# A windowed attention step over both key groups, on half-array tiles

## Chip, cores and metric

The kernel runs on one core of a Trainium2 chip. The metric is the device time of one execution in microseconds (us). Engines are named as in the profile: PE is TensorE (PEld its weight loads), DVE VectorE, ACT ScalarE, POOL GpSimd, SP SyncE, which here issues most DMAs.

## What is computed

A trunk of two layers on one sequence of 1024 tokens, width 1024. Layer 0 mixes tokens by windowed attention, layer 1 by a gated MLP; each is followed by a dense squared-ReLU MLP. The change lies in the attention of layer 0, cut to its core here (CHUNK = 64, 16 chunks, 16 query heads of 64, 2 key heads, so 8 query heads for each; a chunk's queries see their own chunk and the one before, 128 keys):

```
q, k, v = split(h @ w_qkv)
q = rope(rms_norm(q, q_gain), positions);  k = rope(rms_norm(k, k_gain), positions)
scores = einsum('bnqhgd,bnkhd->bnhgqk', q, kk) * HEAD_DIM ** -0.5     # kk: chunk n-1 and n
m = maximum(max(scores), sink)
p = exp(scores - m)
probs = p / (sum(p) + exp(sink - m))
o = einsum('bnhgqk,bnkhd->bqhd', probs, vv)
return o @ w_o
```

## The kernel before

Activations lie transposed, features on partitions and tokens on the free axis. Products with weights are made of three terms from a high and a low part of each operand (w_hi, w_lo, h_hi, h_lo); the inner products of the attention itself are plain fp32. A weight block of 128 output features is a "unit" (`unit`, matmuls at L1404). SP loads it to w_raw, ACT splits off w_hi (L455), POOL w_lo (L381). Units come in pairs. Unit 0 gives k, units 1 to 8 four pairs of q, unit 9 gives v; units 10 to 17 are the output projection, which needs the finished attention in h_hi and h_lo.

A pair j of q holds four heads, its first halves in one unit, its second in the other. DVE turns it by the rotary angles (`turn`, L1098 to L1110), multiplies by the spread head norms (L1117, L1118) and signals q_cs. SP then writes it to q_dram in eight DMAs (`save_q`, L330), since the attention wants heads side by side and the head dimension on partitions. Pairs 0 and 1 are the heads of key group 0, 2 and 3 those of group 1.

The attention is a pipeline of 32 steps t, step t being chunk n = t // 2 and group g = t % 2, with semaphores between engines and the order on each engine written by hand in its `step`:

- SP: `load_q` loads one tile qf, 64 partitions by 512 (8 heads x 64 tokens), for step t once the scores of t - 2 are done; two tiles. All 32 loads stand behind all saves.
- PE: `scores(t+1)` (L1570): four fp32 matmuls with K = 64 rows, stationary 128 queries of two heads, moving 128 keys, into PSUM tile pp[0] or pp[3] (`score_tile`); it waits for the exps of t - 1. `mix` of step t - 3 (L1589): one matmul, moving pt (128 keys x 512 queries), stationary a 128x128 window v_w that holds the values of group g in its own half and zeros in the other, so that both groups add up in one PSUM bank of 128 partitions. `turn` of step t - 2 (L1580): four transposes of the probabilities into pp[1].
- DVE: maxima (L1139), sums and reciprocal of t - 1 (L1128, L1130), the copy of transposed probabilities to pt for group 0 (L1147), the low part of the output once per chunk (L1152). The sinks are written once as a column behind each score row (L1170) and stay there, as each PSUM tile belongs to one group.
- ACT: four exps (L617), the copy to pt for group 1 (L626), the high part of the output (L630), the copy to v_w (L637).
- POOL: normalises the probabilities (L394).

The loop has its first eight and last four steps as straight code, the others in a hardware loop. Ahead of it PE transposes v (L1559), ACT copies that (L605), and DVE waits for all saves of q.

Of the kernel before, what the change touches and what calls it, by code (L numbers as in the profile page):

```python
# [13 lines left out]
S = 1024  # L14
# [22 lines left out]
U_K, U_Q, U_V = 0, 1, KC + 1  # L37
U_WO = KC + 2
# [26 lines left out]
def build(nc, x_in, c_in, pos_in, weights, mod_w, cols, mats, ws_in, bias_in, q_dram, v_dram, out):  # L65
# [5 lines left out]
    with ctx:  # L71
# [31 lines left out]
        with ExitStack() as attn:  # L103
            kf = sb("kf", [HD, KV, PAD + S], f32, attn)
            vt = sb("vt", [P, PAD + S], f32, attn)
            v_s = sb("v_s", [P, NCH, P], f32, attn)
            with ExitStack() as rope:
# [4 lines left out]
                oa = sb("oa", [P, 2, S], f32, rope)  # L112
                ob = sb("ob", [P, 2, S], f32, rope)
            qf = sb("qf", [HD, 2, HALF], f32, attn)
            pr = sb("pr", [P, 4, 4, P + 1], f32, attn)
            pt = sb("pt", [P, 2, HALF], f32, attn)
            v_w = sb("v_w", [P, 2, 3 * P], f32, attn)
            small = sb("small", [P, 4, 4, 4], f32, attn)
# [68 lines left out]
        qf_in = [sem("qf_in0"), sem("qf_in1")]  # L187
# [3 lines left out]
        vw, pv_mm, o_hi, o_lo = (sem(n) for n in ("vw", "pv_mm", "o_hi", "o_lo"))  # L191
        sinks_in, vw_zero = sem("sinks_in"), sem("vw_zero")
# [35 lines left out]
        def score_tile(g):  # L228

            return (pp[0], pp[3])[g][:, :].rearrange("p (a c) -> p a c", a=2)[:, :, 0:2 * (P + 1)].rearrange(  # L230
                "p a (b k) -> p a b k", b=2)

# [39 lines left out]
        def _(sp):  # L272
# [51 lines left out]
            def save_q(j):  # L324

                sp.wait_ge(q_cs, 2 * j + 2)
                for i in range(4):
                    head = 4 * (j % 2) + i
                    for part, src in ((0, oa), (1, ob)):
                        sp.dma_start(q_dram[:, j // 2, 32 * part:32 * part + 32, head, :].rearrange("n d t -> d n t"),  # L330
                                     src[32 * i:32 * i + 32, 1 - j % 2, :].rearrange("d (n t) -> d n t", t=CHUNK)).then_inc(q_out[j], 16)

            with sp.Fori(1, 4) as pair:
                for s in range(2):
                    load_block(pair, s, -1)
            save_q(0)
            load_block(4, 0, -1)
# [4 lines left out]
            save_q(2)  # L342
            save_q(3)

            def load_q(t, n, g):
                if not static(t) or t >= 2:
                    sp.wait_ge(sc_mm, t - 1)
                sp.dma_start(qf[:, g, :], q_dram[n, g]).then_inc(qf_in[g], 16)

            for j in range(4):  # L350
                sp.wait_ge(q_out[j], 16 * 8)
            sp.wait_ge(k_roped, 2)
            for g in range(KV):
                load_q(g, 0, g)
            with sp.Fori(1, NCH) as n:
                for g in range(KV):
                    load_q(n * 2 + g, n, g)
# [20 lines left out]
        def _(pool):  # L378
# [5 lines left out]
            nc.gpsimd.memset(kf[:, 0, 0:PAD], 0.0).then_inc(pads, 1)  # L384
            nc.gpsimd.memset(kf[:, 1, 0:PAD], 0.0).then_inc(d_lo, 1)
            nc.gpsimd.memset(vt[:, 0:PAD], 0.0).then_inc(pads, 1)
            pool.wait_ge(pads, 2)
# [62 lines left out]
        def _(act):  # L450
# [125 lines left out]
            for j in range(4):  # L576
# [7 lines left out]
                if j == 0:  # L584
                    act.wait_ge(k_roped, 2)
                    for g in range(KV):
                        for part in range(2):
                            act.dma_start(kf[32 * part:32 * part + 32, g, PAD:],
# [20 lines left out]
            def exps(t, b):  # L609

                lo = PAD if static(t) and t < 2 else 0
                sc = score_tile(b % 2)
                act.wait_ge(p_max, t + 1)
                if not static(t) or t >= 4:
                    act.wait_ge(p_tr, t - 3)
# [5 lines left out]
            def probs_copy(t, n):  # L621

                act.wait_ge(p_tr, t + 1)
                if not static(t) or t >= 2:
                    act.wait_ge(pv_mm, t - 1)
                nc.scalar.activation(pt[:, 1, :], pp[1][:, HALF:], ACT.Copy).then_inc(p_cp[1], 1)  # L626

            def out_high(n, e):
                act.wait_ge(pv_mm, n * 2 + 2)
                nc.scalar.activation(h_hi[:, :, bass.ds(n * CHUNK, CHUNK)],  # L630
                                     pp[2][:, HALF * e:HALF * e + HALF].rearrange("p (h t) -> p h t", t=CHUNK),
                                     ACT.Copy).then_inc(o_hi, 1)

            def window(n, e):
                if not static(n) or n >= 2:
                    act.wait_ge(pv_mm, n * 2 - 2)
                nc.scalar.activation(v_w[:, e, :].rearrange("p (g c) -> p g c", g=2)[:, :, 0:HD],  # L637
                                     v_s[:, bass.ds(n, 1), :].rearrange("p a (g c) -> p (a g) c", g=KV),
                                     ACT.Copy).then_inc(vw, 1)

            def step(m, b):

                t = m * 4 + b
                if not static(t) or t < 2 * NCH:
                    exps(t, b % 4)
                    if b % 2 == 0:
                        window(m * 2 + b // 2, (b // 2) % 2)
                if b % 2 and (not static(t) or 3 <= t < 2 * NCH + 2):
                    probs_copy(t - 2, m * 2 + ((b - 1) // 2 - 1))
                if b % 2 == 0 and (not static(t) or t >= 4):  # L650
                    out_high(m * 2 + (b // 2 - 2), (b // 2) % 2)

            act.wait_ge(v_cp, 4)
            act.wait_ge(vw_zero, 1)
            for m in range(2):
                for b in range(4):
                    step(m, b)
            with act.Fori(2, NCH // 2 - 1) as m:
                for b in range(4):
                    step(m, b)  # L660
            for b in range(7):
                step(NCH // 2 - 1, b)
# [211 lines left out]
        def _(dve):  # L874
# [217 lines left out]

            for j in range(4):
# [17 lines left out]
                if j == 1:  # L1111
                    mod_part(2)
                if j < 3:
# [7 lines left out]
            mod_part(3)  # L1121


            def sums(t, b):
                dve.wait_ge(p_exp, t + 1)
                if not static(t) or t >= 4:
# [5 lines left out]
            def maxima(t, b):  # L1132

                lo = PAD if static(t) and t < 2 else 0
                sc = score_tile(b % 2)
                dve.wait_ge(sc_mm, t + 1)
                if lo:
                    V.memset(pr[:, b, :, 0:lo], 0.0)
# [3 lines left out]
            def probs_copy(t, n):  # L1142

                dve.wait_ge(p_tr, t + 1)
                if not static(t) or t >= 2:
                    dve.wait_ge(pv_mm, t - 1)
                V.tensor_copy(pt[:, 0, :], pp[1][:, 0:HALF]).then_inc(p_cp[0], 1)  # L1147

            def out_low(n, e):
                cs = bass.ds(n * CHUNK, CHUNK)  # L1150
                dve.wait_ge(o_hi, n + 1)
                V.tensor_tensor(out=h_lo[:, :, cs],  # L1152
                                in0=pp[2][:, HALF * e:HALF * e + HALF].rearrange("p (h t) -> p h t", t=CHUNK),
                                in1=h_hi[:, :, cs].bitcast(f32), op=ALU.subtract).then_inc(o_lo, 1)

            def step(m, b):
                t = m * 4 + b
                if not static(t) or t < 2 * NCH:
                    maxima(t, b % 4)
                if not static(t) or 1 <= t < 2 * NCH + 1:  # L1160
# [659 lines left out]
```

## Time and profile before

| | us |
|---|---|
| median of 3 runs | 2422.3 (2419.77 to 2426.09) |
| profiled execution | 2425.68 |
| its span, first to last instruction | 2423.9 |
| mean granted clock of PE | 0.979 of full speed |
| PE busy | 2313.5 (95%) |
| DVE, ACT, POOL busy | 1222.3, 670.5, 771.4 |
| last q turned to first scores | 200.1 to 214.3 |
| first scores to output projection | 214.3 to 314.1 |

The span holds all instructions of one execution; the rest of its time lies outside. A busy PE isn't a PE at its peak, as a matmul record includes its way through the array and records overlap. So durations of PE work are best read as the distance from start to start. The granted clock says which share of 2.4 GHz the chip gave PE. The attention takes a small part of the span; most is the dense products on both sides of it.

### The profile page before, as it was taken

To read this page: it belongs to the slowest core of one execution; us is meant where nothing else is said; L and a number is where in the kernel's file an instruction comes from. 1 tells how busy PE (TensorE), PEld (TensorE's weight loads), DVE (VectorE), ACT (ScalarE), POOL (GpSimd) and SP (SyncE) were. 2 spreads that over 40 slices of the span, in tenths; PEclk is the share of its full clock that TensorE was granted. 3 is DMA by queue.
4 is the path that set the end of the run, shared out by engine and by line. 5 is a ranking of instruction groups with operands and counts; after the bars stand their busy time and mean duration, and the time that the engine had idled before them with its cause. 6 is when DMAs were issued, how large, how long until landed. Compare 5 with 4: busy or idle time off the path is not lost.

```text
span 2423.9 us, 28984 instructions
## 1 busy us (share of the span) xinstructions
PE 2313.5 (95%) x10184; PEld 1853.6 (76%) x10184; DVE 1222.3 (50%) x1518; ACT 670.5 (28%) x904; POOL 771.4 (32%) x569
## 2 busy tenths in 40 slices
PE   2897998999999999998999999999899999999999
PEld 1686677788888888886788788888678888888887
DVE  7775747656656665436333541343654454445311
ACT  2323622322322332213222221121323223223210
POOL 1121321256445534211211112112153454455211
PEclk8897998999999999998999999999999999999999
DMA  6352241121222122211434221121011111111112
GB/s 255 96 156 67 64 165 44 61 87 53 83 90 69 61 78 87 89 50 35 139 124 133 97 95 44 61 78 44 27 53 44 61 43 52 52 52 43 55 50 87
DMA packets 76753, 189.22 MB, mean 78 GB/s; under 512 B 23440, under 2 KB 25360, under 8 KB 76176
## 3 DMA queue, kind: packets, MB, share of 16 engines
q1 hardware_dynamic: 58288, 127.64, 16.3%
q10 hardware_dynamic: 18400, 60.69, 7.0%
q8 instruction: 43, 0.70, 0.1%
q14 instruction: 22, 0.18, 0.0%
HBM read 170.48 MB, written 16.78 MB: 77 GB/s over the span
## 4 chain that ended last, share of the span: by engine, by line
PE 47%; issue 46%; POOL 6%; POOLq 0%; DVE 0%; ACT 0%; DVEq 0%
PE pp L1404 28%; PE pp L1664 19%; POOL w_lo L381 5%; POOL pr L394 1%; POOL w_lo L420 0%; PE pp L1481 0%; POOLq L440 0%; POOLq L380 0%; DVE x L1198 0%; ACT w_hi L692 0%; POOLq L393 0%; POOLq L398 0%; POOLq L388 0%; POOLq L436 0%; POOLq L424 0%
## 5 line engine op out<-in xcount | busy, mean ns | idle before, releaser
L381 POOL TENSOR_TENSOR w_lo<-w_raw,w_hi 128x1024 fp32r<-128x1024 f32 x146 | 359.0, 2460 | 1332.9 <-ACT w_hi L455 1332.9
L1404 PE MATMUL pp<-h_hi,w_hi 128*128 128x512 f32 x1824 | 599.7, 404 | 41.9 <-DVE h_lo L981 23.0
L1404 PE MATMUL pp<-h_lo,w_hi 128*128 128x512 f32 x1824 | 590.3, 399 | 0.0
L1404 PE MATMUL pp<-h_hi,w_lo 128*128 128x512 f32 x1824 | 590.0, 399 | 0.0
L1404 PEld LDWEIGHTS pp<-h_hi,w_hi 128*128 128x128 f32 x1824 | 342.9, 190 | 133.9 <-issue 21.8
L1404 PEld LDWEIGHTS pp<-h_hi,w_lo 128*128 128x128 f32 x1824 | 347.0, 190 | 84.5
L1404 PEld LDWEIGHTS pp<-h_lo,w_hi 128*128 128x128 f32 x1824 | 347.3, 190 | 82.9
L1268 DVE SCALAR_TENSOR_TENSOR x<-pp,mod,x 128x512 f32<-128x512 f32 x336 | 252.6, 752 | 241.2 <-PE pp L1664 241.2
L455 ACT ACTIVATE w_hi<-w_raw 128x1024 fp32r<-128x1024 f32 x146 | 154.1, 1056 | 641.4 <-PE pp L1404 536.9
L1664 PE MATMUL pp<-c_hi,w_hi 128*128 128x512 f32 x672 | 265.8, 396 | 0.0
L1664 PE MATMUL pp<-c_lo,w_hi 128*128 128x512 f32 x672 | 265.8, 396 | 0.0
L1664 PE MATMUL pp<-c_hi,w_lo 128*128 128x512 f32 x672 | 265.8, 396 | 0.0
L1404 PE MATMUL pp<-hid_hi,w_hi 128*128 128x512 f32 x512 | 166.6, 396 | 0.0
L1404 PE MATMUL pp<-hid_hi,w_lo 128*128 128x512 f32 x512 | 166.0, 395 | 0.0
L1404 PE MATMUL pp<-hid_lo,w_hi 128*128 128x512 f32 x512 | 166.0, 395 | 0.0
L420 POOL TENSOR_TENSOR w_lo<-s_w,w_hi 128x768 fp32r<-128x768 f32 x96 | 122.7, 1295 | 116.3 <-ACT w_hi L692 116.3
L1198 DVE SCALAR_TENSOR_TENSOR x<-pp,mod,x 128x1024 f32 (+1 forms) x34 | 43.5, 1280 | 220.4 <-PE pp L1404 220.4
L1664 PEld LDWEIGHTS pp<-c_lo,w_hi 128*128 128x128 f32 x672 | 126.3, 188 | 30.5
L1664 PEld LDWEIGHTS pp<-c_hi,w_hi 128*128 128x128 f32 x672 | 126.3, 188 | 30.5
L1664 PEld LDWEIGHTS pp<-c_hi,w_lo 128*128 128x128 f32 x672 | 126.3, 188 | 30.4
L1216 DVE SCALAR_TENSOR_TENSOR c_f<-pp,tmp 128x512 f32<-128x512 f32 x72 | 47.5, 688 | 197.0 <-ACT tmp L699 197.0
L420 POOL TENSOR_TENSOR w_lo<-w_raw,w_hi 128x256 fp32r<-128x256 f32 x96 | 97.7, 1018 | 105.0 <-ACT w_hi L692 102.1
(159 smaller groups left out, 2273.1 us busy)
## 6 DMA issues: line engine op xcount, KB each, us to landing
w_raw<-weights SPq DMA_DIRECT2D x194, 512.0 KB, 3.5
mod_t<-mod_w ACTq DMA_DIRECT2D x64, 512.0 KB, 4.1
mod_first<-mod_w SPq DMA_DIRECT2D x16, 512.0 KB, 15.4
mod_late<-mod_w ACTq DMA_DIRECT2D x2, 4096.0 KB, 19.8
v_dram<-v_out ACTq DMA_DIRECT2D x16, 512.0 KB, 5.4
vf<-v_dram ACTq DMA_DIRECT2D x16, 512.0 KB, 3.3
x<-x_in SPq DMA_DIRECT2D x4, 1024.0 KB, 8.7
qf<-q_dram SPq DMA_DIRECT2D x32, 128.0 KB, 2.5
```

What stands on the lines that cost most here:

```text
L381: nc.gpsimd.tensor_tensor(out=w_lo[:, s, :, :], in0=w_raw[:, s, :, :], in1=w_hi[:, s, :, :].bitcast(f32), op=ALU.subtract).then_inc(lo_don ...
L394: nc.gpsimd.tensor_tensor(out=pr[:, b, :, 0:P], in0=pr[:, b, :, 0:P], in1=small[:, b, 3, :].unsqueeze(2).to_broadcast([P, 4, P]), op=ALU.m ...
L420: nc.gpsimd.tensor_tensor(out=down_target(w_lo, part), in0=down_source(part, q), in1=down_target(w_hi, part).bitcast(f32), op=ALU.subtract ...
L455: nc.scalar.activation(w_hi[:, s, :, :], w_raw[:, s, :, :], ACT.Copy).then_inc(hi_done, 1)
L1198: V.scalar_tensor_tensor(out=xn, in0=pp[s][:, :], scalar=mod[:, gate, bass.ds(i * 2 + s, 1)], in1=xn, op0=ALU.mult, op1=ALU.add).then_inc( ...
L1216: V.scalar_tensor_tensor(out=out, in0=src[:, columns_of(half)], scalar=0.0, in1=tmp[:, s, columns_of(half)], op0=ALU.max, op1=ALU.mult).th ...
L1268: V.scalar_tensor_tensor(out=xn, in0=banks[BANK[t]], scalar=mod[:, 6 * layer + GATE2, 2 * q + m:2 * q + m + 1], in1=xn, op0=ALU.mult, op1= ...
L1404: last = T.matmul((pp[s] if tile is None else tile)[:, cs], w[:, s, k, :], r[:, k, cs], start=(k == 0 and w is w_hi and r is hi), stop=(k ...
L1664: last = T.matmul(banks[BANK[t]], w[:, slot, k, :], r[:, i, OPERAND[t], :], start=(t in FRESH and i == 0 and w is w_hi and r is c_hi), sto ...
```

## The change

All 32 steps stay, but a step now is one chunk for both key groups and half of the heads: step t is chunk t % 16, and t // 16 says which half (four heads of each group).

- Order of the q pairs: `Q_ORDER` makes pair 0 and 1 the first half of the heads of group 0 and group 1, pair 2 and 3 the second. SP loads the weight blocks accordingly, and `save_q` writes accordingly.
- SP: four `load_q` are issued ahead of the last save, after the saves of pairs 0 and 1 and the last turn of q; loads 4 to 15 after it; loads 16 to 31 after the saves of pairs 2 and 3. qf is 128 partitions by 256, four tiles, so load t waits for the scores of t - 3.
- Scores: four matmuls with K = 64, two on rows 0 to 63 (group 0) and two on rows 64 to 127 (group 1), by turns, each group into its own PSUM bank. kf is 128 partitions high for it.
- Mixing: two matmuls with 64 stationary columns and 256 moving ones, group 0 to PSUM partitions 0 to 63 and group 1 to 64 to 127. They read v_s; v_w, its memset and its copies go. A bank is full after two steps (two chunks), as before.
- Copies to pt: DVE for one step in four, ACT for three (before: half each).
- Sinks: DVE writes those of the first half before the last multiplications of q (behind `mod_part(3)`, which moves there too), and those of the second half at steps 16 and 17, after the exps of the step two before.
- PE issues `scores(0)` ahead of the V transposes. All loops of the attention are straight code but POOL's.
- oa and ob no longer share memory with what the loop uses.

```diff
             for j in range(2):
+                sp.wait_ge(q_out[j], 16 * 8)
+            sp.wait_ge(q_turned, 4)
+            for t in range(4):
+                load_q(t)
             save_q(3)
...
+            for t in range(4, NCH):
+                load_q(t)
+            for j in range(2, 4):
                 sp.wait_ge(q_out[j], 16 * 8)
+            for t in range(NCH, STEPS):
+                load_q(t)
...
+        def copied_by_vector(t):
+
+            return t % 4 == 0
...
+                if j == 3:
+                    mod_part(3)
+                    dve.wait_ge(evac[0], U_WO // 2)
+                    for t in range(2):
+                        sinks(t, 0)
...
+            for t in range(STEPS + 4):
+                if t in (NCH, NCH + 1):
+                    dve.wait_ge(p_exp, t - 1)
+                    sinks(t, 1)
+                if t < STEPS:
+                    maxima(t)
+                if 1 <= t < STEPS + 1:
+                    sums(t - 1)
+                if 2 <= t < STEPS + 2 and copied_by_vector(t - 2):
+                    probs_copy(t - 2)
+                if t % 2 and t >= 5:
+                    out_low((t - 1) // 2 - 2)
...
+                for r in range(2):
+                    for g in range(KV):
+                        rows = slice(HD * g, HD * g + HD)
+                        last = T.matmul(score_tile(t)[:, g, r, 0:P], qf[rows, t % 4, P * r:P * r + P], kf[rows, keys],
+                                        start=True, stop=True)
...
+                at = HALF * (u % 2) + 2 * P * (t % 2)
+                for g in range(KV):
+                    rows = slice(HD * g, HD * g + HD)
+                    last = T.matmul(pp[2][rows, at:at + 2 * P], v_s[:, t % NCH, rows], pt[:, t % 2, 2 * P * g:2 * P * g + 2 * P],
+                                    start=True, stop=True)
...
+            for t in range(STEPS + 3):
+                if t + 1 < STEPS:
+                    scores(t + 1)
+                if t == 2:
+                    pe.wait_ge(v_cp, 4)
+                if 3 <= t < STEPS + 3:
+                    mix(t - 3)
+                if 2 <= t < STEPS + 2:
+                    turn(t - 2)
```

## Rows read from the trace of the kernel before

**Rows 1.** Table by stage: stretch, its us, busy of each engine, granted clock, DMA.

```profile
207.00:208.00 1.00, 0.00 (x0) 0.00 (x0) 0.00 (x0) 0.00 (x0) 0.00 (x0) 0.54 0.90 187
...
234.00:235.00 1.00, 1.00 (x8) 1.00 (x8) 0.94 (x2) 0.00 (x1) 0.00 (x0) 0.80 0.00 0
...
240.00:250.00 10.00, 9.66 (x53) 6.35 (x51) 7.57 (x16) 6.67 (x21) 3.94 (x4) 1.00 0.15 40
```

**Rows 2.** Timeline, 198 to 220 us: start, duration, engine, line, operation [idle before, releaser].

```profile
198.84 1.22 DVE L1110 TENSOR_TENSOR ob<-ob,qa 128x1024 f32<-128x1024 f32 x1
...
201.03 1.09 PE L1559 MATMUL pp<-ident,vt 128*128 128x128 f32 x8 [0.24 <-ACT vt L601]
...
202.03 1.21 DVE L1118 TENSOR_TENSOR ob<-ob,pp 128x1024 f32<-128x1024 f32 x1
...
203.15 1.08 ACT L605 ACTIVATE v_s<-pp 128x512 f32<-128x512 f32 x2 [0.26 <-PE pp L1559]
203.16 1.22 DVE L905 TENSOR_REDUCE col_sum<-pp 128x8 f32<-128x1024 f32 x1
203.27 0.32 SPq L330 DMA_DIRECT2D q_dram<-oa  x1
...
205.69 0.23 DVE L1170 COPY pp<-colt 128x4 f32<-128x4 f32 x2
...
207.85 0.73 SPq L330 DMA_DIRECT2D q_dram<-ob  x1
...
211.59 20.22 SPq L348 DMA_DIRECT2D qf<-q_dram  x8
...
214.33 3.75 PE L1570 MATMUL pp<-kf,qf 64*128 64x128 f32 x16 [10.72 <-DMA qf<-q_dram]
...
217.14 1.28 ACT L617 ACT_TABLE_LOAD   x1 [12.91 <-DVE small L1139]
...
218.44 0.93 ACT L617 ACTIVATE pr<-pp,small 128x65 f32<-128x65 f32 x4
```

**Rows 3.** Timeline of the steady loop, 258 to 264 us, full clock.

```profile
258.28 1.15 PE L1570 MATMUL pp<-kf,qf 64*128 x8 [0.24 <-ACT pr L617]
...
259.36 1.12 PE L1589 MATMUL pp<-pt,v_w 128*128 128x512 f32 x2
...
260.32 0.60 PE L1580 MATMUL pp<-ident,pr 128*128 128x128 f32 x4
...
260.85 1.16 PE L1570 MATMUL pp<-kf,qf 64*128 x8
260.96 0.69 DVE L1147 COPY pt<-pp 128x512 f32<-128x512 f32 x1 [1.10 <-PE pp L1580]
...
262.29 1.15 ACT L617 ACTIVATE pr<-pp,small 128x129 f32<-128x129 f32 x4 [0.88 <-DVE small L1139]
...
263.59 1.15 PE L1570 MATMUL pp<-kf,qf 64*128 x8
```

**Rows 4.** Chain of work in order of time, two normalisations four steps apart: start, us.

```profile
247.00 1.04 POOL pr L394
...
257.77 1.04 POOL pr L394
```

**Rows 5.** Timeline of the first steps, at the lower clock: two scores that follow.

```profile
224.24 2.07 PE L1570 MATMUL pp<-kf,qf 64*128 64x128 f32 x8
...
229.10 2.07 PE L1570 MATMUL pp<-kf,qf 64*128 64x128 f32 x8
```

**Rows 6.** Groups by line and shape, 236 to 300 us: busy, mean ns, idle before.

```profile
L626 ACT ACTIVATE pt<-pp 128x512 f32<-128x512 f32 x12 | 7.2, 597 | 0.9 <-PE pp L1580 0.3
```

**Rows 7.** Timeline near 168 us: head sums, matmuls with 4 moving columns.

```profile
167.83 1.84 PE L1488 MATMUL pp<-colt,tmp 128*128 128x4 f32 x16
```

**Rows 8.** Timeline of the loop's end, 301 to 315 us.

```profile
301.15 1.13 PE L1570 MATMUL pp<-kf,qf 64*128 64x128 f32 x8
...
314.14 0.70 PE L1404 MATMUL pp<-h_hi,w_hi 128*128 128x512 f32 x2 [1.60 <-DVE h_lo L1152]
```

More of the change, by code:

```diff
@@ L634, in window @@
[L634 to L662, printed above, removed]
+                nc.scalar.activation(pt[:, t % 2, :], pp[1][:, columns_of(t % 2)], ACT.Copy).then_inc(p_cp[t % 2], 1)
+            def out_high(u):
+                act.wait_ge(pv_mm, u * 2 + 2)
+                nc.scalar.activation(out_tokens(h_hi, u), out_bank(u), ACT.Copy).then_inc(o_hi, 1)
@@ L1090, in _, with sinks @@
             mods(2)
+            def sinks(t, half):
+                V.tensor_copy(score_tile(t)[:, :, :, P:P + 1],
+                              colt[:, sink0:sink0 + 8].rearrange("p (g a r k) -> p g a r k", g=KV, a=2, k=1)[:, :, half, :, :]
+                              ).then_inc(sinks_in, 1)
             for j in range(4):
@@ L1120, in _, with sums @@
                     mods(2)
-            mod_part(3)
-            def sums(t, b):
+            def sums(t):
+                b = t % 4
                 dve.wait_ge(p_exp, t + 1)
-                if not static(t) or t >= 4:
+                if t >= 4:
                     dve.wait_ge(p_norm, t - 3)
@@ L1156, in step @@
[L1156 to L1160, printed above, removed]
-                    sums(t - 1, (b + 3) % 4)
-                if b % 2 == 0 and (not static(t) or 2 <= t < 2 * NCH + 2):
-                    probs_copy(t - 2, m * 2 + (b // 2 - 1))
-                if b % 2 and (not static(t) or t >= 5):
-                    out_low(m * 2 + ((b - 1) // 2 - 2), ((b - 1) // 2) % 2)
@@ L1177, in _, with out_low @@
-            for m in range(2):
-                for b in range(4):
-                    step(m, b)
-            with dve.Fori(2, NCH // 2 - 1) as m:
-                for b in range(4):
-                    step(m, b)
-            for b in range(8):
-                step(NCH // 2 - 1, b)
+                V.tensor_copy(pt[:, t % 2, :], pp[1][:, columns_of(t % 2)]).then_inc(p_cp[t % 2], 1)
+            def out_low(u):
+                dve.wait_ge(o_hi, u + 1)
+                V.tensor_tensor(out=out_tokens(h_lo, u), in0=out_bank(u), in1=out_tokens(h_hi, u).bitcast(f32),
+                                op=ALU.subtract).then_inc(o_lo, 1)
@@ L1561, in _ @@
                 last.then_inc(v_tr, 1)
-            pe.wait_ge(v_cp, 4)
-            def scores(t, n, g):
-                pe.wait_ge(qf_in[g], n * 16 + 16)
-                if not static(t) or t >= 2:
-                    pe.wait_ge(p_exp, t - 1)
-                for r in range(4):
-                    last = T.matmul(score_tile(g)[:, r // 2, r % 2, 0:P], qf[:, g, P * r:P * r + P],
-                                    kf[:, g, bass.ds(n * CHUNK, P)], start=True, stop=True)
-                last.then_inc(sc_mm, 1)
@@ L1603, in _ @@
-            pe.wait_ge(evac[1], U_WO // 2)
-            scores(0, 0, 0)
-            for m in range(2):
-                for b in range(4):
-                    step(m, b)
-            with pe.Fori(2, NCH // 2 - 1) as m:
-                for b in range(4):
-                    step(m, b)
-            for b in range(7):
-                step(NCH // 2 - 1, b)
+            for t in range(STEPS + 3):
+                if t + 1 < STEPS:
[6 more added lines that the diff above has]
+                    turn(t - 2)
```

176 lines of the change are left out of this document (82 added, 94 removed).

## The prediction

> **What bounds the kernel now.** I read four views, in this order. The page's busy shares put PE far ahead of all others, so what counts is the stretches in which PE isn't fed; the change touches 200 to 314 us. The table by stage: the granted clock is at its lower level (0.50, 1.2 GHz) from 207 to 208 on and is back (1.00, 2.4 GHz) only within 234 to 235, well inside the attention loop; in the loop's steady part PE is busy 9.66 of 10 us [rows 1]. The timeline from 198 to 220 shows what the loop waits for: PE idles 10.72 for the first query tile, which SP issues at 211.59, behind the eight saves of the last q pair [rows 2]. The timeline of the steady loop shows the steps: the POOL normalisations of 247.00 and 257.77 are four steps apart, so a step is 10.77/4 = 2.69 us [rows 3, 4].
>
> Who sets 2.69? PE's own work is scores 259.36 - 258.28 = 1.08, mixing 260.32 - 259.36 = 0.96, transposes 260.85 - 260.32 = 0.53, together 2.57. A loop through all engines is as long: scores 1.08, mixing 0.96, 0.64 from the first transpose to DVE's copy (260.96), 1.33 through copy and maxima to the exps (262.29), 1.30 to the scores two steps on (263.59): 5.31, or 2.65 a step [rows 3]. So both must shrink for a step to shrink. In the slow clock PE alone sets it: 229.10 - 224.24 = 4.86, 1.89 times its 2.57 [rows 3, 5].
>
> **The change, part by part.**
>
> *Earlier start.* The first sixteen steps need only the first two q pairs, saved long before, so four query loads go ahead of save 3 on SP and wait for the last turn of q. That turn (L1110) ends at 198.84 + 1.22 = 200.06; issue to the first scores took 214.33 - 211.59 = 2.74; so the tile is there at 202.8 [rows 2]. On DVE mod_part(3) and the two sink copies now stand ahead of the last two multiplications: 205.69 + 0.23 - 203.16 = 2.76, so sinks are in at 202.8 as well, scores(0) starts at 202.9 and ends at 204.0. The multiplications (two of 1.2) end at 205.2, the small memset and first maxima before 206. ACT comes later: its V copies now follow scores(0), and transposes and copies took 201.03 to 203.15 + 1.08 = 204.23, 3.2 us; so 207.2, then the table load, 218.44 - 217.14 = 1.3. First exps at 208.5 in place of 218.44, 9.9 earlier [rows 2]. Late next is SP: save 3 waits for the multiplications, its eight issues take 207.85 + 0.73 - 203.27 = 5.3, and load 4 stands behind them: issued at 210.6, landed at 213.3. So scores(4) starts at 213.3; before, it started at 224.24 [rows 2, 5]. Loads 16 to 31 wait for saves 2 and 3, long landed; the ring of four tiles hides a load behind four steps. The weight loads behind them on SP lie over 10 us ahead of their use, as before, and cost nothing; if that cover went they'd delay the output projection by their landing time.
>
> *Scores by array rows.* Four matmuls as before, but the two groups use rows 0 to 63 and 64 to 127. Each fp32 matmul is two records (x8 for a step's four), and records follow each other at 1.08/8 = 0.135 [rows 3]. The trace of before has no two matmuls side by side, so I bound it. Above: nothing overlaps, 1.08. A nearer bound is the weight load: matmuls with only 4 moving columns still take 1.84/16 = 0.115 each [rows 7], so if loads go one by one, 8 x 0.115 = 0.92. Below: records stay in order, the second of one group beside the first of the next, five slots of 0.135 = 0.68. I take 0.80, between the last two.
>
> *Mixing by array columns.* One 128x512 matmul (two records of 0.48) becomes two with 64 output columns and 256 moving: four records of 0.24. One by one 0.96; in order with the middle pair side by side three slots, 0.72. Transposes are now at another shape than the mixing: 1.08 - 0.92 = 0.16 is the most that these rows leave for going to another shape, so 0.72 to 0.96 plus up to 0.16; I take 0.80. The zero-padded value window goes, and with it a small ACT copy and a wait on ACT once per chunk; the mixings follow the scores without idle time ahead of them, so I count zero [rows 3].
>
> The Trainium skill ("TensorEngine Tiling (Array Packing)", Key Properties) says that changing the tiling mode drains TensorE. Of that a row shows at most the 0.16 above; by the page the changed loop pays a third drain in each step, and with 0.16 in full the pace would be 2.48 in place of 2.40.
>
> *Copies.* DVE copies the probabilities in one step of four, ACT in three. The loop then is, for the step with DVE's copy, 5.31 - 2.04 + s + m = 3.27 + s + m; for the other even step, with ACT's copy (0.60) and the high output (as large, 0.6 as an estimate) ahead of the exps, s + m + 0.64 + 0.60 + 0.60 + 1.30 = 3.14 + s + m [rows 3, 6]. Four steps: 6.41 + 2(s + m). With s = m = 0.80: 9.61, a pace of 2.40. DVE is busy 7.57 of 10 us, 2.04 a step, and loses a quarter of a copy, ACT 6.67, 1.79, and swaps the window copy for a quarter copy, so neither sets it, though DVE is close [rows 1].
>
> *Second sinks.* At steps 16 and 17 the new sink copies stand behind DVE's sums, and scores 16 and 17 wait for them: an estimate of 1.3 each, the 1.33 that a copy and a maxima take together: 2.6. Queued behind them on PE: a mixing and a transpose each, and with those ACT's copies. The loops become straight code; the first eight steps were straight code before, and no row shows a wait for it: zero.
>
> *The clock.* PE will again be thinly used from 204 to 213, and I expect the clock to fall there: it fell in 207 to 208 in such a hole [rows 1]. Before, it came back 15.9 after the first exps; I take the same, 224.4. Slow pace: PE's 0.80 + 0.80 + 0.53 by the 1.89 of above, 4.03.
>
> **Sum.** scores(4) at 213.3; (224.4 - 213.3)/4.03 = 2.75 steps; the other 24.25 to scores(31) at 2.40: 58.2, so 282.6; second sinks 2.6: 285.2. From the last scores to the output projection it was 314.14 - 301.15 = 13.0 [rows 8]; with shorter mixing 12.5: 297.7. Gain 314.1 - 297.7 = 16.4. The profiled execution took 2425.7 (1.8 outside its span): 2409.3. It is 3.4 above the median of the three runs (2422.3), so in terms of that median 2406.
>
> **The rivals.**
>
> *The array doesn't overlap (the change doesn't do what it says).* s + m is 2.04, the loop 10.49 for four steps, 2.62; PE with a third change of shape needs 2.57 to 2.73; I take 2.65. Slow steps at 4.86: 2.3 done by 224.4; 24.7 x 2.65 = 65.5, + 2.6 + 13.0: 305.5, gain 8.6, 2414. At 2.73 it is 6.7, 2416. For it: the spacing of matmuls with 4 columns [rows 7]; against: nothing in the trace.
>
> *Full overlap, weight loads included.* s 0.54 (but ACT's copy then holds the mixing back to an effective 0.66), m 0.50: (6.41 + 2.32)/4 = 2.18; slow pace 1.57 x 1.89, about 3.0. 3.7 slow steps, 23.3 x 2.18 = 50.8, + 2.6 + 12: 289.8, gain 24.3: 2398. The Trainium skill (same page, Key Properties) says that tiles load weights and multiply in parallel; no row here shows two records at once.
>
> *The clock doesn't fall.* 27 x 2.40 = 64.8 from 213.3, + 2.6 + 12.5: 293.2, gain 20.9: 2401. For it: scores and V transposes now lie in what was the hole.
>
> *The clock stays low: slower.* Before it rose, PE had worked through half-height scores, full-array mixing and transposes, and was still at the lower level at 229, with the loop running since 224 [rows 1, 5]. The changed loop has no full-array fp32 matmul left; if half-array work doesn't bring the clock back, all 27 steps cost 4.03: 109, so scores(31) at 322, + 4 + 17: 343, 29 later than before, 2451 (2474 at 4.86). It decides from 16.4/(4.03 - 2.40) = 10 slow steps beyond the 2.75 assumed, that is with the clock low until about 265.
>
> **How the numbers follow.** Forecast 0.37, no overlap 0.24, full overlap 0.10, clock never falls 0.08, clock stays low 0.21. About 0.3% (7.3 us) is what a measurement of this kernel can tell from no change; the no-overlap case straddles it, and I split it 0.13 and 0.11. Faster: 0.37 + 0.10 + 0.08 + 0.13 = 0.68; same 0.11; slower 0.21. The range leaves out most of the low-clock case only: from 2395, under full overlap, to 2432, which takes in no overlap with a late return of the clock.
>
> **What would show it.** First scores at about 203 and first exps near 208.5; scores(4) behind a load at about 213; scores of a step in 0.7 to 0.9 at the full clock, mixing in 0.7 to 0.9; a pace of 2.3 to 2.5 between normalisations; a hole at steps 16 and 17; the granted clock low for some 15 us only. A pace near 2.65 says the array does nothing side by side; a granted clock of 0.50 beyond 265 overturns the sign. The output projection should start at about 297, and all after it be unchanged. What would make the forecast wrong outside these: a new wait in the fill between 203 and 213, where three engines trade places.

## The result, and the profile after

The changed kernel takes 2401.88 us (median of five runs, 2398.36 to 2408.17), the kernel before, on the same chip, 2422.87 (2419.77 to 2426.09): a ratio of 0.9917, 95% interval 0.9904 to 0.9929. That is 21.0 us less, or 0.83%, 4.1 us under the forecast of 2406.0. The profiled execution took 2401.88, with a span of 2400.1; against the profiled one of before (span 2423.9) the gain is 23.8. Of these 23.8, 2.3 were there before the attention began: the copy of V into vt, which closes the part that both kernels share, starts that much earlier (before, then after, with the granted clock of one stretch ahead of it):

```profile
100.00:120.00 20.00, 17.14 (x62) 14.02 (x62) 13.96 (x11) 3.35 (x4) 2.67 (x1) 0.67 0.42 131
...
199.95 1.02 ACT L601 ACTIVATE vt<-pp 128x1024 f32<-128x1024 f32 x1 [2.47 <-PE pp L1404]
```

```profile
100.00:120.00 20.00, 17.12 (x68) 13.84 (x67) 15.38 (x12) 3.36 (x4) 2.67 (x1) 0.77 0.40 129
...
197.63 1.02 ACT L623 ACTIVATE vt<-pp 128x1024 f32<-128x1024 f32 x1 [2.47 <-PE pp L1399]
```

The change leaves PE's work there as it was. Over all twelve profiled executions of this study this copy starts between 196.30 and 200.62, and the later, the lower the granted clock from 100 to 140 was (0.92 for 196.30, 0.89 for 197.63, 0.81 for 199.95, 0.80 for 200.62). So times of two profiles are best compared from this copy on.

Now the table by stage, as [rows 1] (stretch, its us, busy time of PE, PEld, DVE, ACT and POOL with their instructions, granted clock, DMA share, GB/s):

```profile
207.00:208.00 1.00, 0.14 (x2) 0.17 (x4) 0.25 (x1) 1.00 (x6) 0.00 (x0) 1.00 0.96 195
208.00:214.00 6.00, 5.55 (x33) 3.69 (x34) 4.85 (x11) 3.05 (x11) 2.69 (x3) 0.51 0.59 154
214.00:215.00 1.00, 1.00 (x6) 0.67 (x7) 0.67 (x2) 0.03 (x1) 0.65 (x2) 0.54 0.35 116
215.00:216.00 1.00, 0.97 (x12) 0.59 (x12) 0.36 (x1) 1.00 (x4) 0.82 (x1) 1.00 0.00 0
...
242.00:245.00 3.00, 3.00 (x20) 1.83 (x16) 1.39 (x5) 0.80 (x3) 1.04 (x1) 0.54 0.13 44
...
287.00:290.00 3.00, 3.00 (x9) 2.32 (x8) 0.04 (x1) 0.00 (x0) 0.00 (x0) 0.50 0.91 287
```

The clock is at its lower level in four short stretches: three and a half us under the V transposes (0.57 from 201 to 205), about seven while the loop starts, three in its middle, three and a half behind its end. Before, it was low from 207 to 234 without a break [rows 1].

The timeline of the fill, which answers to [rows 2]:

```profile
197.85 1.76 SPq L357 DMA_DIRECT2D qf<-q_dram  x4
...
200.51 0.71 PE L1556 MATMUL pp<-kf,qf 64*128 64x128 f32 x8 [2.04 <-DVE pp L1094]
...
201.15 3.68 PE L1591 MATMUL pp<-ident,vt 128*128 128x128 f32 x16
...
205.49 1.28 ACT L640 ACT_TABLE_LOAD   x1
...
206.78 1.97 ACT L640 ACTIVATE pr<-pp,small 128x65 f32<-128x65 f32 x8
...
208.40 9.47 SPq L357 DMA_DIRECT2D qf<-q_dram  x7
...
211.62 1.22 PE L1556 MATMUL pp<-kf,qf 64*128 64x128 f32 x8 [0.45 <-DMA qf<-q_dram]
```

What was a wait of 10.72 us for a query tile [rows 2] is gone: the first scores stand at 200.51 and now wait for DVE's sink copies, the first exponentials at 206.78 and not 218.44. The load for step 4 is still issued late (at 208.40, behind the eight saves of the last pair), but PE waits only 0.45 for it.

Then the steady loop, as [rows 3, 4]; the two groups are PE's one step, and DVE's two copies of the probabilities, which are four steps apart:

```profile
227.90 0.71 PE L1556 MATMUL pp<-kf,qf 64*128 64x128 f32 x8 [0.32 <-ACT pr L640]
228.54 0.65 PE L1577 MATMUL pp<-pt,v_s 128*64 128x256 f32 x4
229.13 0.66 PE L1566 MATMUL pp<-ident,pr 128*128 128x128 f32 x4
229.71 0.71 PE L1556 MATMUL pp<-kf,qf 64*128 64x128 f32 x8
```

```profile
221.09 0.69 DVE L1161 COPY pt<-pp 128x512 f32<-128x512 f32 x1 [0.97 <-PE pp L1566]
...
229.82 0.69 DVE L1161 COPY pt<-pp 128x512 f32<-128x512 f32 x1 [0.97 <-PE pp L1566]
```

Start to start, the scores take 0.64 (before: 1.08), the mixing 0.59 (0.96), the transposes 0.58 (0.53). Four steps take 229.82 - 221.09 = 8.73, a pace of 2.18 in place of 2.69.

Around the second sinks:

```profile
237.85 0.66 PE L1566 MATMUL pp<-ident,pr 128*128 128x128 f32 x4
241.44 0.71 PE L1556 MATMUL pp<-kf,qf 64*128 64x128 f32 x8 [2.94 <-DVE pp L1094]
242.09 1.03 PE L1577 MATMUL pp<-pt,v_s 128*64 128x256 f32 x4
243.04 1.12 PE L1566 MATMUL pp<-ident,pr 128*128 128x128 f32 x4
```

PE waits 2.94 for the sink copy, and right after, the same transposes take 1.12 and not 0.66: the clock has fallen. DVE's copies on either side of it stand at 238.54 and 250.89, 12.35 for four steps in place of 8.73: the second sinks cost 3.6.

And the end, as [rows 8]:

```profile
275.16 0.71 PE L1556 MATMUL pp<-kf,qf 64*128 64x128 f32 x8 [0.32 <-ACT pr L640]
...
286.21 0.85 PE L1399 MATMUL pp<-h_hi,w_hi 128*128 128x512 f32 x2 [1.61 <-DVE h_lo L1165]
```

The output projection starts at 286.21, 27.9 earlier than before (314.14). From there the kernel takes 2400.1 - 286.2 = 2113.9, before 2423.9 - 314.1 = 2109.8. So 4 us of the gain are given back. The stretch at 0.50 behind the start of the projection explains 1.6 of them (the first five pairs of matmuls take 290.16 - 286.21 = 3.95, where the pairs behind them start 0.47 apart, which would be 2.34). Following the same instruction in both traces finds the rest: ScalarE's split of one weight block starts at 1683.67 before and 1657.78 after, still 25.9 apart, and of another, a hundred us on, at 1792.14 and 1768.34, 23.8 apart as at the end. So 2.1 were lost in that one stretch, and 0.4 between the two. The clock there, before, then after:

```profile
1720.00:1740.00 20.00, 13.23 (x49) 10.14 (x48) 13.84 (x20) 6.64 (x10) 2.35 (x1) 0.83 0.10 34
```

```profile
1700.00:1720.00 20.00, 17.19 (x63) 13.57 (x64) 12.62 (x20) 6.00 (x9) 0.00 (x0) 0.75 0.06 26
1720.00:1740.00 20.00, 16.65 (x62) 12.19 (x61) 14.99 (x19) 9.82 (x11) 4.91 (x2) 0.91 0.17 54
```

From 1680 to 1760 the clock's lower level took about 7 us before and 14 after. The work there is the same in both kernels, and 7 us more at half the clock can cost up to 3.4.

### The profile page after: what moved, and what is told of

The parts are those of the page before. It is cut to its first block, busy times and chain, and to the rows that moved or that the text cites. A ratio compares the mean times of both kernels' runs of the same rounds, so it can differ in the third digit from the quotient of the medians.

```text
span 2400.1 us, 28782 instructions
## 1 busy us (share of the span) xinstructions
PE 2289.4 (95%) x10248; PEld 1832.3 (76%) x10248; DVE 1216.6 (51%) x1511; ACT 669.3 (28%) x896; POOL 772.1 (32%) x568
## 4 chain that ended last, share of the span: by engine, by line
PE 48%; issue 46%; POOL 6%; POOLq 0%; DVE 0%; ACT 0%; DVEq 0%
PE pp L1399 29%; PE pp L1654 19%; POOL w_lo L403 5%; POOL pr L416 1%; POOL w_lo L442 0%; PE pp L1476 0%; POOLq L462 0%; POOLq L402 0%; DVE x L1193 0%; ACT w_hi L691 0%; POOLq L415 0%; POOLq L420 0%; POOLq L410 0%; POOLq L458 0%; POOLq L446 0%
```

## The experiments

The times are medians. They were taken in four series, each on one chip beside runs of the kernel before, whose medians were 2422.9 to 2424.0. "Pace" is us for one of the 32 steps at the full clock, from normalisations or copies four steps apart. "Stage" is read from the one profiled execution of each kernel: us from the start of the copy of V into vt to the start of the output projection, which leaves out what the clock did elsewhere. For the kernel before it is 314.14 - 199.95 = 114.2.

| kernel | us | ratio to before (95%) | pace | stage |
|---|---|---|---|---|
| changed kernel | 2401.9 | 0.9917 (0.9904 to 0.9929) | 2.18 | 88.6 |
| norow: scores not by rows | 2455.1 | 1.0133 (1.0115 to 1.0150) | 4.10, all at 1.2 GHz | 144.4 |
| nocol: mixing not by columns | 2406.0 | 0.9924 (0.9907 to 0.9941) | 2.35 | 97.6 |
| neither | 2418.2 | 0.9980 (0.9970 to 0.9990) | 2.61 | 111.1 |
| late: no early loads | 2416.3 | 0.9967 (0.9952 to 0.9982) | 2.18 | 104.2 |
| order: scores group by group | 2403.2 | 0.9913 (0.9895 to 0.9931) | 2.18 | 92.8 |
| norow_more: norow, transposes twice | 2423.9 | 1.0001 (0.9992 to 1.0010) | 2.69 | 112.0 |
| sinks: both sinks at the start | 2395.3 | 0.9888 (0.9872 to 0.9905) | 2.18 | 84.8 |
| turnfirst: transposes before mixing | 2393.8 | 0.9870 (0.9846 to 0.9895) | 1.99 | 84.5 |
| best: sinks and turnfirst | 2390.5 | 0.9863 (0.9847 to 0.9880) | 1.99 | 78.7 |
| scalarcopy: best, copies all on ScalarE | 2385.6 | 0.9844 (0.9831 to 0.9858) | 1.85 | 76.3 |

### Undoing one tiling, the other, or both

**norow** keeps the order, the ring of four and the tiled mixing, but holds the queries and keys of both groups on partitions 0 to 63, so that the scores can't run beside each other.

```diff
-            kf = sb("kf", [P, PAD + S], f32, attn)
+            kf = sb("kf", [HD, KV, PAD + S], f32, attn)
...
-                        last = T.matmul(score_tile(t)[:, g, r, 0:P], qf[rows, t % 4, P * r:P * r + P], kf[rows, keys],
+                        last = T.matmul(score_tile(t)[:, g, r, 0:P], qf[:, t % 4, g, P * r:P * r + P], kf[:, g, keys],
```

> The changed kernel with both key groups' queries and keys on partitions 0 to 63, so that the four score matmuls of a step share their rows; all else as changed. If the array works on both halves at once (the changed kernel shows scores start to mixing start 0.64, mixing to transposes 0.59), scores go back to 1.08 a step, and the loop 6.41 + 2(1.08 + 0.59) = 9.75 for four steps gives a pace of 2.44 in place of 2.18: some 7 us slower than the changed kernel, about 2409. If scores only looked shorter because records are drawn differently, the time stays at 2402. If half-height work alone can't bring the clock back, the lower clock lasts beyond 230 and it is over 2412.

It is 32 us slower than the kernel before, and 46 slower than the 2409 expected if only the overlap went. Two stretches of the table by stage and four lines of its timeline:

```profile
216.00:240.00 24.00, 24.00 (x95) 16.13 (x95) 11.28 (x22) 10.27 (x31) 6.07 (x6) 0.50 0.12 33
...
346.00:347.00 1.00, 1.00 (x6) 0.78 (x6) 0.00 (x0) 0.00 (x0) 0.00 (x0) 1.00 1.04 430
```

```profile
251.83 2.07 PE L1556 MATMUL pp<-kf,qf 64*128 64x128 f32 x8
253.83 1.12 PE L1577 MATMUL pp<-pt,v_s 128*64 128x256 f32 x4
254.88 1.12 PE L1566 MATMUL pp<-ident,pr 128*128 128x128 f32 x4
255.93 2.07 PE L1556 MATMUL pp<-kf,qf 64*128 64x128 f32 x8
```

PE is busy 24.00 of 24.00 us and the clock stays at 0.50; it stays there from 206 until the output projection runs. A step takes 255.93 - 251.83 = 4.10. This is the rival of the slower side as it was written, in a kernel beside the one it was written for.

**nocol** keeps the tiled scores and gives the mixing back its zero-padded windows of 128 columns. The zeros cost VectorE one memset more (0.91 us) ahead of the sinks.

```diff
-                    last = T.matmul(pp[2][rows, at:at + 2 * P], v_s[:, t % NCH, rows], pt[:, t % 2, 2 * P * g:2 * P * g + 2 * P],
-                                    start=True, stop=True)
+                    last = T.matmul(pp[2][:, at:at + 2 * P], v_s[:, t % NCH, HD * g:HD * g + P], pt[:, t % 2, 2 * P * g:2 * P * g + 2 * P],
+                                    start=g == 0, stop=g == 1)
```

> The changed kernel with full 128-column stationary windows for the mixing (values of one group beside zeros, both groups added up in the bank), two matmuls of 256 moving columns as before; all else as changed, and one memset of about 0.9 us more ahead of the sinks. If column tiles overlap, mixing goes from 0.59 to 0.96 a step, the loop 6.41 + 2(0.64 + 0.96) = 9.61: pace 2.40, some 6 to 7 us slower than changed, about 2409. If they don't, it stays at 2402 to 2403. If full-array mixing is what brings the clock back, its low stretch in the fill is shorter here than the 7 us of the changed kernel.

Its timeline in the steady loop:

```profile
255.43 0.71 PE L1557 MATMUL pp<-kf,qf 64*128 64x128 f32 x8
256.28 1.13 PE L1578 MATMUL pp<-pt,v_s 128*128 128x256 f32 x4
257.25 0.60 PE L1567 MATMUL pp<-ident,pr 128*128 128x128 f32 x4
```

The mixing takes 257.25 - 256.28 = 0.97, its untiled time, the scores still 0.7; four steps take 9.38. The column tiles are worth 0.16 a step, and the medians differ by 4 us where 6 to 7 were expected; the intervals of the two ratios overlap, so the total alone would not show it. In the profiles the stage is 9.0 us longer. The clock at the start of the loop is low from 209 to 216, as long as in the changed kernel, so full-array mixing didn't bring it back sooner here.

**neither** undoes both (with the same memset) and leaves the early start, the order of the steps and the ring.

> Both undone: only the new order of heads, the earlier start, the ring of four and the copy split are left. My theory: pace 2.60 to 2.65 as before, so the loop gives back 27 x 0.45 = 12 and the earlier start stays: 2414, 8 to 9 faster than before; if the low clock in the fill lasts as long as before, 2417. The rival, that the gain is mostly the earlier start, wants it under 2407.

The pace is 2.61 (two normalisations, at 275.83 and 286.27), the time 2418.2, 1 above the higher of the two times expected. So without tiles the new order is worth under 5 us, though the first exponentials, at 209.47, come 9.0 us sooner than before [rows 2] (2.2 of them had been gained ahead of the attention). They run in a loop that the lower clock slows for most of the time until 225, and the second sinks, which the kernel before doesn't have, take more back: from scores(12) at 240.21 to scores(20) at 267.14 pass 26.9 us, where eight steps of 2.61 are 20.9.

**late** keeps the tiles and puts all loads of queries behind all saves, as before.

```diff
-            for j in range(2):
+            save_q(3)
+            for j in range(4):
                 sp.wait_ge(q_out[j], 16 * 8)
             sp.wait_ge(q_turned, 4)
-            for t in range(4):
-                load_q(t)
-            save_q(3)
...
-            for t in range(NCH, STEPS):
+            for t in range(STEPS):
                 load_q(t)
```

> The changed kernel with all 32 query loads behind all four saves and their landing, as before; tiles kept. First scores at about 211 (2.3 earlier than before at most), so the start is given back: first exps some 9 later, at 216. Theory: 2402 + 9 = 2411, and up to 3 more if the clock falls in the wider hole and stays low longer. If the start were hidden anyway it would be 2402 to 2404.

```profile
216.41 1.22 PE L1550 MATMUL pp<-kf,qf 64*128 64x128 f32 x8 [14.96 <-DMA qf<-q_dram]
217.56 3.77 PE L1585 MATMUL pp<-ident,vt 128*128 128x128 f32 x16
...
225.23 1.04 POOL L410 TENSOR_TENSOR pr<-pr,small 128x512 f32<-128x512 f32 x1 [20.21 <-DVE small L1135]
```

PE's wait is back, and longer (14.96), because the V transposes, which used to fill part of it, now stand behind scores(0). The first normalisation is at 225.23, in the changed kernel at 208.73: 16.5 later. Of this 3.0 is no work of the edit: V's copy already starts at 200.62, under a lower clock than the changed kernel had before its attention. The other 13.5 are. The medians differ by 14.4, 2 to 5 more than was expected, with late's runs spread from 2409.6 to 2419.7. The early loads are so worth some 14 us once the tiles are there, and the tiles 16 once the loads are early.

### Whether the tiles depend on the order of issue

In the changed kernel neighbouring score matmuls alternate between the row tiles. **order** issues both of group 0, then both of group 1.

```diff
-                for r in range(2):
-                    for g in range(KV):
+                for g in range(KV):
+                    for r in range(2):
```

> The scores' matmuls are issued group by group (both row tiles of heads of group 0, then both of group 1) and not in turn; nothing else differs. Theory A, that row tiles overlap only where two neighbouring instructions sit on different rows: of the four matmuls only the middle two are such neighbours, so the scores cost about 0.80 and not 0.64, the loop of four steps is longer by 2 x 0.16 = 0.3, the pace of a step 2.26 for 2.18, 32 steps 2.6 us more: about 2404.5, and the granted clock may take longer to come back. Theory B, that the engine works through each row tile's queue by itself: pace 2.18 and the time that of the changed kernel, about 2402.

```profile
227.88 0.72 PE L1556 MATMUL pp<-kf,qf 64*128 64x128 f32 x8 [0.31 <-ACT pr L640]
228.54 0.65 PE L1577 MATMUL pp<-pt,v_s 128*64 128x256 f32 x4
```

The scores take 0.66 where they took 0.64, the pace is the same 2.18, and 2403.2 lies within the changed kernel's runs. Theory B holds: over four matmuls, a tile doesn't wait for its neighbour in the program to be of the other tile. The clock did stay low for longer in this profile (the changed kernel has 0.79 in both of these stretches):

```profile
240.00:248.00 8.00, 6.55 (x39) 4.12 (x40) 4.12 (x12) 2.77 (x10) 2.49 (x3) 0.57 0.10 33
...
284.00:292.00 8.00, 5.70 (x18) 3.26 (x19) 2.29 (x3) 1.46 (x3) 0.00 (x0) 0.50 0.20 41
```

That makes its stage 4.2 us longer at the same pace. Whether the order of issue or chance did it, one profile of each can't tell; the medians differ by 1.3 only.

### What holds the clock down

norow left open whether its clock stays low because of what its matmuls are, or for another reason, since the engine is busy all the time. **norow_more** is norow with every transpose done twice.

```diff
-                for r in range(4):
+                for r in [0, 1, 2, 3] * 2:
                     at = HALF * (t % 2) + P * r
```

> The kernel with scores not tiled by rows (norow) and one thing more: each step's four transposes are done twice, to the same place, so that TensorE has 1.05 us more of work a step at the clock of 1.2 GHz that norow had throughout, and it is work on the whole array. Theory A (norow's clock stays at 1.2 GHz because its matmuls, scores on half of the rows one after the other and mixing on half of the columns, are too light a use of the array, however full the engine's busy share): the clock comes back to 1.00 in the stage, the pace falls from 4.10 to about 2.7 in spite of the added work, and the time from 2455 to about 2415. Theory B (the clock stays low for another reason, for one that the engine is never idle there): the pace rises by 1.05 to about 5.15, and the time to about 2489.

```profile
208.00:223.00 15.00, 14.69 (x61) 11.87 (x62) 7.27 (x16) 5.14 (x18) 4.62 (x5) 0.50 0.23 66
...
224.00:225.00 1.00, 1.00 (x10) 0.88 (x11) 0.00 (x0) 1.00 (x3) 0.00 (x0) 1.00 0.00 0
```

```profile
229.17 1.16 PE L1556 MATMUL pp<-kf,qf 64*128 64x128 f32 x8
230.26 0.65 PE L1577 MATMUL pp<-pt,v_s 128*64 128x256 f32 x4
230.84 1.09 PE L1566 MATMUL pp<-ident,pr 128*128 128x128 f32 x8
231.90 1.13 PE L1556 MATMUL pp<-kf,qf 64*128 64x128 f32 x8
```

With more work per step the kernel is 31 us faster: the clock is back at 224, and a step with eight transposes takes 2.69 to 2.73 where one with four took 4.10. Theory A's pace came out, its time didn't: 2423.9 is 9 above the 2415 expected. So it isn't how busy the engine is by the profile that keeps norow at 1.2 GHz, but which matmuls fill it. What exactly the chip looks at these runs don't tell.

The same rows carry a second reading: 0.58 for the tiled mixing (230.84 - 230.26) beside untiled scores of 1.09. The tiled mixing is as fast without its tiled neighbour.

### What the changed kernel still waits for

**sinks** writes the sink columns of both halves before the first scores (a score row has 130 cells, a sink at either end, and each half reads 129 of them; the padding of the first chunk is set to a large negative number ahead of the maxima).

```diff
-                if t in (NCH, NCH + 1):
-                    dve.wait_ge(p_exp, t - 1)
-                    sinks(t, 1)
...
-                if t in (0, 1, NCH, NCH + 1):
-                    pe.wait_ge(sinks_in, 2 * (t // NCH) + t % NCH + 1)
+                if t < 2:
+                    pe.wait_ge(sinks_in, 2 * t + 2)
```

> Both columns of sinks are written before the first scores, so that no wait for the exponentials of step 15 stands in the middle of the stage; scores have 130 cells a head, and the maxima, exponentials and sums read 129 of them. Theory A (the hole of about 3.8 us near 241 and the clock's fall to 1.2 GHz behind it are what the wait costs): the four steps around step 16 take about 8.7 as the others do, the granted clock stays at 1.0 there, and the time falls by 3.8 plus under 1: about 2397.5. Theory B (the hole is made up for elsewhere, or the memset of the pads in the middle of the stage takes its place): 2401 to 2402.

```profile
242.00:245.00 3.00, 2.65 (x26) 1.85 (x28) 2.94 (x6) 2.94 (x10) 1.87 (x2) 1.00 0.20 59
```

In the stretch in which the changed kernel ran at 0.54 the clock is now 1.00, and the stage is 88.58 - 84.82 = 3.8 us shorter: Theory A, to the amount. The medians differ by 6.6 where 4.4 was expected; in the profiles the difference beyond the stage lies in parts that the edit doesn't touch, 1.0 ahead of V's copy and 2.1 near 1700 us, where the changed kernel's clock was low for longer.

**turnfirst** swaps two calls in PE's loop, so that the transposes of step t - 2 no longer stand behind the mixing of step t - 3.

```diff
-                if 3 <= t < STEPS + 3:
-                    mix(t - 3)
                 if 2 <= t < STEPS + 2:
                     turn(t - 2)
+                if 3 <= t < STEPS + 3:
+                    mix(t - 3)
```

> TensorE issues the transposes of step t-2 ahead of the mixing of step t-3, and not behind it; nothing else differs. Theory A (the pace of 2.18 is a loop of four steps that runs through scores, mixing and transposes in TensorE's order, with the mixing's time in it twice): the mixing leaves the loop, which is (8.73 - 2 x 0.59) / 4 = 1.89 a step, and VectorE with its 2.0 to 2.1 of work a step sets the pace: 2.05 for 2.18, 32 steps 4 us less, about 2398. Theory B (the pace is that of the whole of TensorE's and VectorE's work and not of that loop): pace 2.15 to 2.18, about 2402, or up to 2404 if the mixing now holds the out_low of VectorE back.

The busy time of four steady steps, first of the changed kernel, then of turnfirst:

```profile
225.26:233.99 8.73, 7.54 (x67) 4.66 (x65) 7.44 (x16) 7.00 (x23) 4.17 (x5) 1.00 0.20 63
```

```profile
224.98:232.94 7.96, 7.49 (x68) 4.66 (x64) 7.43 (x16) 6.92 (x23) 4.17 (x4) 1.00 0.24 67
```

The work is the same, the time 0.77 shorter: the pace of 2.18 was a chain through PE's order, not the work of any engine. The pace of 1.99 lies between the 1.89 of the loop and the 2.05 expected from DVE; what sets it was not shown. The medians differ by 8.1, twice what was expected, but turnfirst's runs go from 2387.5 to 2397.8, and by the profiles the stage is 88.58 - 84.51 = 4.1 shorter: the faster pace, less what the clock took back (0.57 from 240 to 248, where the changed kernel had 0.79). So the swap is worth between 4 and 8.

**best** has both edits.

> Both edits at once, the sinks of both halves written at the start and the transposes ahead of the mixing. If both causes hold and add: 2401.9 - 4.4 - 4 = about 2393.5. If VectorE is the bound of both: about 2396. If neither holds: 2402.

2390.5: 11.4 below the changed kernel, and 3 better than what the sum of both was expected to give; but less than the 14.7 that the two medians gave one by one. The stages don't show such a loss: 9.9 shorter with both, 3.8 and 4.1 with one.

**scalarcopy** adds one line to best: no step's copy is VectorE's.

```diff
         def copied_by_vector(t):
-            return t % 4 == 0
+            return False
```

> Both edits of best and one more: ScalarE makes all the copies of the transposed weights, where VectorE made every fourth. In best's four steps of 7.96 VectorE is busy for 7.43, ScalarE 6.92, TensorE 7.50. Theory A (the engine with the most work sets the pace): VectorE falls to 6.74 and ScalarE rises to 7.53, four steps take 7.6 to 7.7, 32 steps 2 to 3 us less than best: about 2388. Theory B (a step's chain across the engines sets it, and ScalarE's copies now delay its exponentials): the pace stays at 1.99 or rises to 2.1: 2390 to 2394.

Its four steady steps:

```profile
227.63:235.04 7.41, 7.39 (x67) 4.62 (x65) 6.84 (x15) 7.41 (x24) 4.16 (x4) 1.00 0.22 74
```

Now ScalarE is busy 7.41 of 7.41 and PE 7.39: here, alone among the kernels with both tilings, an engine is full, and the pace is 1.85. ScalarE is the likelier of the two, as PE's parts at the full clock sum to 1.81 a step. Four steps of 7.6 to 7.7 were expected, and 2388. At 2385.6 it is the fastest kernel of the study, 16.3 below the changed one and 1.6% below the one before.

## Why the prediction was right, and where its terms were off

The time and the sign were right, by the mechanisms named: an earlier start, narrower scores and mixing. But the forecast's output projection at 297.7 was 11.5 late against 286.2, and the closeness of the time is in part luck. Behind the start of the projection 4.1 were lost again, nearly all by the clock, which leaves 7.4 (2409.3 forecast for the profiled execution, 2401.9 measured). Another 3.4 had been taken off because the profiled execution of before lay above its median; the changed kernel's profiled execution is its median. The stage came out nearest to the rival of full overlap (projection at 289.8, chance 0.10), the time between the forecast and that rival's 2398. Term by term:

**Earlier start: right.** Forecast for scores(4) 213.3, measured 211.62; first exponentials 208.5, measured 206.78. Both are 1.7 earlier than forecast, but only because all that stands ahead is 2.3 earlier than before, by the clock. Counted from the end of the last turn of q (forecast 200.06, measured 196.53 + 1.23 = 197.76), the first scores come after 2.75 (forecast 2.84), the first exponentials after 9.02 (forecast 8.44). The 0.6 too much is V's transposes and copies: 201.15 to 205.47, 4.3 and not 3.2, as the clock fell there too. The step "late next is SP" held: load 4 is issued behind the saves, and PE waits 0.45 for it. late shows the worth of the whole edit, some 14.

**Scores 0.80 and mixing 0.80: the terms that were mis-sized.** They are 0.64 and 0.59. This is the rival of full overlap (0.66 in effect, 0.50), to which the prediction gave 0.10, and its pace of 2.18 is the measured one, by two errors that cancel: its s + m was 0.07 too small, and the formula of the loop gives 0.14 too much for four steps. The step that failed is the choice "between the last two" bounds, the 0.92 of weight loads one by one and the 0.68 of records in order. [rows 7] were taken as a price that loads pay in any place; the row is of untiled matmuls, and says nothing of tiles side by side. Eight score records in 0.64 are under both bounds. The second bound assumed that a tile's work waits for the program's order; by that rule the order of issue of the run order would take seven slots, 0.95, and it took 0.66. The 0.22 in the pace over 27 steps is 5.9 of the 11.5.

The Trainium skill (TensorEngine Tiling (Array Packing), Key Properties) says that tiles load weights and multiply in parallel; by the 0.64 the trace agrees. Its rule that a change of the tiling mode drains TensorE is not contradicted. What the third change in a step costs is not shown apart: the transposes take 0.58 where they took 0.53, and the mixing's 0.59 is 0.10 over half of its untiled 0.97, so at most the 0.16 weighed ahead. In norow_more, with the same three shapes, eight transposes take 1.06, and nothing is added to them.

**The loop: right.** 6.41 + 2(s + m) with the measured 0.64 and 0.59 is 8.87, measured 8.73; for nocol (0.65 and 0.97) 9.65, measured 9.38; for neither (1.09 and 0.97) 10.53, measured 10.44. It is 0.1 to 0.3 too long each time. turnfirst took one part of the loop out and the pace followed, with no engine's work changed.

**The clock: half right.** That it would fall in the fill was right; it fell twice, at 201 and at 208. Its return was taken from before, 15.9 after the first exponentials, and came 8 after. The forecast had 2.75 x (4.03 - 2.40) = 4.5 for the slow steps; from scores(4) to scores(31) it was 275.16 - 211.62 = 63.5, which is 27 x 2.18 = 58.9, 3.6 for the sinks and 1.0 for the clock. That is 3.5 of the 11.5. The rival in which it stays low did not happen in the changed kernel, but norow shows that it was no idle fear: the mixing tiled alone is 53 us slower than both tiled, and 37 slower than neither. The argument "half-array work doesn't bring the clock back" was right for score matmuls one after the other beside column-tiled mixing (norow), and wrong for two tiles at once.

**Second sinks 2.6: too small.** 3.6, of which 2.94 is PE's wait and the rest the low clock behind it, which the prediction left out. That clock follows on holes was in [rows 1]; the same rule should have been put on this hole as on the fill. Tail: 12.5, measured 11.05 (275.16 to 286.21).

The terms add up: start 1.7 (2.3 of clock ahead of the attention, less 0.6), pace 5.9, clock 3.5, tail 1.4, less 1.0 for the sinks, are the 11.5.

**"All after it be unchanged": wrong.** From the start of the projection on it took 4.1 more: 1.6 by the clock at 0.50 from 287 to 290, 2.1 between 1658 and 1768, where the lower level lasted twice as long as before, and 0.4 between the two. How long the clock stays low there differs between profiles whose code there is the same (sinks has 0.96 from 1680 to 1760, best 0.91), so this part isn't the change's.

## What to carry to other kernels

Two half-array matmuls on different row or column tiles take about a fifth more than the time of one (0.64 for four scores where one after the other took 1.08), loads included, and here in either order of issue; but check the clock when tiling only one of two neighbours, since serial half-height matmuls beside column-tiled ones ran at 1.2 GHz throughout. When no engine is full and the pace is still a loop, write the loop down with its terms, and look at which instruction stands behind which in a queue: a swap of two calls took 0.19 us off every step, and a single hole of 3 us in mid-stage cost 3.8. Price a hole at its length and the clock's fall behind it. And before a difference of a few us between two profiles is explained, compare the granted clock of the parts that are the same in both: here it moved the start of the attention by up to 4.3 us.

## What was unexpected of the hardware

- More work made a kernel faster: norow with four transposes more in each step went from 2455.1 to 2423.9, by the granted clock alone (0.50 throughout, against 1.00 from 224 on).
- A PE that the profile shows busy for 24.00 of 24.00 us can stay at the lower level of its clock; in norow that level lasted from 206 to about 345.
- Eight fp32 score records on two row tiles take 0.64, which is 0.08 a record, less than the 0.115 that a record with 4 moving columns takes untiled [rows 7].
- A hole of 2.94 us was followed by three us at the lower level (0.54), and the idle tail by three and a half (0.50). The lengths aren't fixed: in order the same hole (2.93) came with seven us at the lower level (0.62 from 240 to 241, 0.50 from 241 to 247) and the tail with thirteen (0.51 from 282 to 295), and before, the clock stayed at 1.00 through the tail and the start of the projection.
- Granted clock before the attention, in code that all the changed kernels share, differed from profile to profile (0.80 to 0.92 from 100 to 140), and with it the attention's start by up to 4.3 us.
